# A three-product split of fp32 matmuls in the FFN's gate and up: two of the three products share weights and are issued as one of 512 columns

## The reference, cut to what matters

```
def swiglu(h, w_gate, w_up, w_down):
    return (jax.nn.silu(h @ w_gate) * (h @ w_up)) @ w_down

for layer in range(2):            # first_block; second_block has the same frame
    x = x + 0.5 * swiglu(rmsnorm(x, g0), w_gate0, w_up0, w_down0)
    x = x + mixer(rmsnorm(x, g1), ...)
    x = x + 0.5 * swiglu(rmsnorm(x, g2), w_gate1, w_up1, w_down1)
```

## Time and profile before

| | |
|---|---|
| median of 3 runs | 2746.84 us (2746.75 to 2747.86) |
| the profiled execution | 2741.84 us |
| its span, first to last instruction | 2740.0 us |
| TensorE busy | 2712.2 us, 99%, 20056 products |
| VectorE busy | 1792.1 us, 65% |
| ScalarE busy | 1430.4 us, 52% |
| GpSimd busy | 291.4 us, 11% |
| DMA | 462.02 MB, mean 169 GB/s |

### The profile page before, as it was taken

The page is one execution under the profiler, slowest core; times in us unless marked ns, Lnnn a source line. Parts: engine busy times, 40 slices in busy tenths (PEclk is TensorE's granted clock), DMA queues, the critical chain, the costliest instruction groups (busy, mean ns, idle before and its releaser), DMA issues.

```text
span 2740.0 us, 49011 instructions
## 1 busy us (share of the span) xinstructions
PE 2712.2 (99%) x20056; PEld 2564.4 (94%) x20056; DVE 1792.1 (65%) x3060; ACT 1430.4 (52%) x2445; POOL 291.4 (11%) x446
## 2 busy tenths in 40 slices
PE   9999999999999999999999999999999999999999
PEld 8999999999999999999998999999999989999998
DVE  6558776556568776556568887565565588975654
ACT  5446554444455555445447675454454476754543
POOL 0005211000005220000004011100000040211000
PEclk9999999999999999999999999999999999999999
DMA  5454334454554345445444334544544442345443
GB/s 210 185 193 159 140 142 177 188 190 171 188 191 154 139 141 185 185 170 198 186 160 168 109 131 164 185 172 185 190 179 185 166 165 108 139 169 185 162 189 142
DMA packets 64733, 462.02 MB, mean 169 GB/s; under 512 B 7296, under 2 KB 7808, under 8 KB 9344
## 3 DMA queue, kind: packets, MB, share of 16 engines
q1 hardware_dynamic: 64512, 458.90, 45.5%
HBM read 457.83 MB, written 1.05 MB: 167 GB/s over the span
## 4 chain that ended last, share of the span: by engine, by line
PE 95%; DVE 2%; POOL 2%; ACT 1%; issue 0%; DMA 0%; SPq 0%; DVEq 0%; POOLq 0%; ACTq 0%
PE bank L423 18%; PE bank L425 18%; PE bank L424 18%; PE bank L501 18%; PE bank L434 4%; PE bank L436 4%; PE bank L435 4%; PE bank L693 2%; POOL MTA L3558 1%; PE bank L605 1%; PE bank L467 1%; PE bank L1113 1%; PE bank L1058 0%; PE bank L639 0%; PE bank L965 0%
## 5 line engine op out<-in xcount | busy, mean ns | idle before, releaser
L2383 DVE TENSOR_TENSOR WLO<-RAW,WHI 128x1024 fp32r<-128x1024 f32 (+1 forms) x872 | 1048.6, 1241 | 223.2 <-ACT WHI L1468 222.5
L423 PE MATMUL bank<-XH,WHI 128*128 128x256 f32 x3712 | 1066.3, 287 | 1.5 <-ACT STB L2004 1.5
L424 PE MATMUL bank<-XL,WHI 128*128 128x256 f32 x3712 | 1051.4, 283 | 0.0
L425 PE MATMUL bank<-XH,WLO 128*128 128x256 f32 x3712 | 1051.4, 283 | 0.0
L1468 ACT CAST WHI<-RAW 128x1024 fp32r<-128x1024 f32 (+1 forms) x872 | 882.8, 1046 | 304.8 <-DMA RAW<-weights_dram 175.5
L423 PEld LDWEIGHTS bank<-XH,WHI 128*128 128x128 f32 x3712 | 712.7, 192 | 12.4 <-issue 3.8
L424 PEld LDWEIGHTS bank<-XL,WHI 128*128 128x128 f32 x3712 | 713.1, 192 | 7.0 <-issue 1.9
L425 PEld LDWEIGHTS bank<-XH,WLO 128*128 128x128 f32 x3712 | 712.7, 192 | 0.0
L1532 ACT ACTIVATE SG<-bank 128x256 f32<-128x256 f32 x152 | 58.4, 384 | 483.0 <-PE bank L425 483.0
L2496 DVE TENSOR_TENSOR HF<-SG,bank 128x256 f32<-128x256 f32 x152 | 63.9, 420 | 337.4 <-ACT SG L1532 337.4
L434 PE MATMUL bank<-WHI,XH 128*128 128x256 f32 (+2 forms) x928 | 267.3, 288 | 4.6 <-DVE XL L2437 4.5
(11 more groups left out here) (346 smaller groups left out, 3185.3 us busy)
## 6 DMA issues: line engine op xcount, KB each, us to landing
RAW<-weights_dram SPq DMA_DIRECT2D x431, 1024.0 KB, 4.8
RAW<-weights_dram SPq DMA_DIRECT2D x2, 800.0 KB, 4.2
X<-x_dram SPq DMA_DIRECT2D x2, 512.0 KB, 5.8
RAW<-weights_dram SPq DMA_DIRECT2D x2, 512.0 KB, 7.1
out_dram<-X SPq DMA_DIRECT2D x2, 512.0 KB, 2.6
RAW<-weights_dram SPq DMA_DIRECT2D x2, 384.0 KB, 3.2
CM<-mixer_dram SPq DMA_DIRECT2D x2, 320.5 KB, 9.7
CM<-mixer_dram SPq DMA_DIRECT2D x2, 176.0 KB, 5.6
```

The lines of the kernel that those rows point to most:

```text
L423: self.e.matmul(bank, h, xh[:, x0 + k, :], start=k == k0, stop=False)
L424: self.e.matmul(bank, h, xl[:, x0 + k, :], start=False, stop=False)
L425: ins = self.e.matmul(bank, l, xh[:, x0 + k, :], start=False, stop=k == k1)
L2383: e.tensor_tensor(WLO[:, c % NLO, a:b], RAW[:, c % NLO, a:b], WHI[:, c % NHI, a:b].bitcast(F32), ALU.subtract).then_inc(*up("lo", c, p))
```

## The change

1. The tokens' high and low parts lie side by side in one tile `XHL`, 512 columns per block of inputs; `XH` and `XL` are its halves.
2. `gu` calls a new helper, `beside`: per block one product of 512 columns (high weights on high and low tokens) and one of 256 (low weights on high tokens). Columns 0 to 255 of the bank hold high x high + low x high, columns 256 to 511 high x low. Gate and up now take a bank each: 4 and 5 for odd slices, 6 and 7 for even ones.
3. The halves are summed on the way out: ScalarE copies the right half to SBUF (`gcopy`, `ucopy`), VectorE adds the left half (`fg`, `fu`); `sg` and `hf` read the sums.
4. The calls of both mixers stand in another order on all four engines, and with them the order of some chunks.

```
-    XH = sb("XH", [P, 8, 256], F32R)
-    XL = sb("XL", [P, 8, 256], F32R)
+    XHL = sb("XHL", [P, 8, 512], F32R)
+    XH, XL = XHL[:, :, 0:256], XHL[:, :, 256:512]
...
+    GS = sb("GS", [P, 2, 256], F32, at_kb(24))
+    VS = sb("VS", [P, 2, 256], F32, at_kb(26))
...
+    def gu_bank(i):
+        return 4 if i % 2 else 6
...
+        def beside(self, bank, c, col, ks, xhl, k0, k1):
+            for k in ks:
+                a = col + k * P
+                h, l = WHI[:, c % NHI, a:a + P], WLO[:, c % NLO, a:a + P]
+                if k == k1:
+                    self.e.matmul(bank[:, 0:256], l, xhl[:, k, 0:256], start=False, stop=False)
+                    ins = self.e.matmul(bank[:, :], h, xhl[:, k, :], start=False, stop=True)
+                else:
+                    self.e.matmul(bank[:, :], h, xhl[:, k, :], start=k == k0, stop=False)
+                    ins = self.e.matmul(bank[:, 0:256], l, xhl[:, k, 0:256], start=False, stop=False)
+            return ins
...
         def gu(self, n, i, g, u):
-            e, c, b = self.e, ck(n, "gu", i), 5 - i % 2
-            if g == u == 0:
-                e.wait_ge(*(at("hf", n, i - 2) if i > 4 else at("ffhid", n, i - 3)))
+            e, c, b = self.e, ck(n, "gu", i), gu_bank(i) + g
             if u == 0:
+                if i > 4:
+                    e.wait_ge(*at("fg" if g == 0 else "fu", n, i - 2))
+                elif b < 7:
+                    e.wait_ge(*at("ffhid", n, b - 4))
+                else:
+                    e.wait_ge(*at("ffl", n, 2))
                 e.wait_ge(*at("lo", c, g))
-            ins = self.pairs(PS[b][:, g * 256:g * 256 + 256], c, g * 1024, range(4 * u, 4 * u + 4), XH, XL, 0, 0, 7)
+            ins = self.beside(PS[b], c, g * 1024, range(4 * u, 4 * u + 4), XHL, 0, 7)
...
+        def gcopy(self, n, i):
+            e.wait_ge(*at("gu", n, i, 0, 1))
+            e.copy(GS[:, i % 2, :], PS[gu_bank(i)][:, 256:512]).then_inc(*up("gcopy", n, i))
+        def ucopy(self, n, i):
+            e.wait_ge(*at("gu", n, i, 1, 1))
+            if i > 4:
+                e.wait_ge(*at("hf", n, i - 2))
+            e.copy(VS[:, i % 2, :], PS[gu_bank(i) + 1][:, 256:512]).then_inc(*up("ucopy", n, i))
         def sg(self, n, i):
-            e.wait_ge(*at("gu", n, i, 1, 1))
+            e.wait_ge(*at("fg", n, i))
-            e.activation(SG[:, i % 2, :], PS[5 - i % 2][:, 0:256], ACT.Silu).then_inc(*up("sg", n, i))
+            e.activation(SG[:, i % 2, :], GS[:, i % 2, :], ACT.Silu).then_inc(*up("sg", n, i))
...
+        def fg(self, n, i):
+            e.wait_ge(*at("gcopy", n, i))
+            e.tensor_tensor(GS[:, r, :], GS[:, r, :], PS[gu_bank(i)][:, 0:256], ALU.add).then_inc(*up("fg", n, i))
+        def fu(self, n, i):
+            e.wait_ge(*at("ucopy", n, i))
+            e.tensor_tensor(VS[:, r, :], VS[:, r, :], PS[gu_bank(i) + 1][:, 0:256], ALU.add).then_inc(*up("fu", n, i))
...
-M2_ORDER = [("bt", 0), ("bt", 1), ("bt", 2), ("bt", 3), ("bx", 9), ("bq", 0), ("bq", 1), ("bq", 2), ("bk", 0), ("bx", 0), ("bx", 10),
+M2_ORDER = [("bt", 0), ("bt", 1), ("bt", 2), ("bt", 3), ("bx", 9), ("bq", 0), ("bq", 1), ("bx", 0), ("bq", 2), ("bx", 10), ("bk", 0),
```

More of the change, by code:

```diff
@@ L747, in m1 @@
             self.ptr(n, 9)
+            self.at_(n, 12, 0, 0)
+            self.at_(n, 12, 0, 1)
+            self.at_(n, 12, 1, 0)
+            self.at_(n, 12, 1, 1)
+            self.at_(n, 5, 0, 0)
+            self.sc(n, 0, 0)
+            self.sc(n, 0, 1)
+            self.at_(n, 5, 0, 1)
+            self.at_(n, 5, 1, 0)
+            self.at_(n, 5, 1, 1)
             self.at_(n, 10, 0, 0)
@@ L1577, in ffn @@
             self.ffh(n, 2)
+            self.gcopy(n, 3)
             self.sg(n, 3)
+            self.ucopy(n, 3)
             self.hh(n, 3)
@@ L1581, in ffn @@
             self.hi(c + 7, 1)
-            for m in range(2, 11):
+            for m in range(2, 10):
                 k = c + 3 * m
-                if m < 10:
-                    self.hi(k + 2, 0)
-                else:
-                    self.hi(k + 1, 1)
+                self.hi(k + 2, 0)
+                self.gcopy(n, 2 * m)
                 self.sg(n, 2 * m)
+                self.ucopy(n, 2 * m)
                 self.hh(n, 2 * m)
-                if m < 10:
-                    self.hi(k + 2, 1)
-                    self.sg(n, 2 * m + 1)
-                    self.hi(k + 3, 0)
-                    self.hh(n, 2 * m + 1)
-                    self.hi(k + 3, 1)
-                    self.hi(k + 4, 0)
-                    if m < 9:
-                        self.hi(k + 4, 1)
-                else:
-                    self.hi(k + 2, 0)
-                    self.hi(k + 2, 1)
-                    self.sg(n, 21)
-                    self.hh(n, 21)
+                self.hi(k + 2, 1)
+                self.gcopy(n, 2 * m + 1)
+                self.sg(n, 2 * m + 1)
+                self.hi(k + 3, 0)
+                self.ucopy(n, 2 * m + 1)
+                self.hh(n, 2 * m + 1)
+                self.hi(k + 3, 1)
+                self.hi(k + 4, 0)
+                if m < 9:
+                    self.hi(k + 4, 1)
                 if n == 0 and 4 <= m < 8:
                     self.tab(1 + (m - 4) // 2, m % 2)
-            self.hi(first[n + 1], 0)
-            self.hi(first[n + 1], 1)
+            self.gcopy(n, 20)
+            self.hi(c + 31, 1)
+            self.sg(n, 20)
+            self.hi(c + 32, 0)
+            self.ucopy(n, 20)
+            self.gcopy(n, 21)
+            self.hh(n, 20)
+            self.hi(c + 32, 1)
+            self.sg(n, 21)
+            self.ucopy(n, 21)
+            self.hi(c + 33, 0)
+            self.hh(n, 21)
+            self.hi(c + 33, 1)
         def psq(self, n, j):
@@ L2546, in ffn @@
             self.lo(c + 7, 1)
[L2547 removed]
+            for m in range(2, 10):
                 k = c + 3 * m
[L2549 to L2552 removed]
+                self.lo(k + 2, 0)
+                self.fg(n, 2 * m)
+                self.fu(n, 2 * m)
                 self.hf(n, 2 * m)
                 self.hl(n, 2 * m)
[L2555 to L2568 removed]
+                self.lo(k + 2, 1)
+                self.fg(n, 2 * m + 1)
+                self.fu(n, 2 * m + 1)
+                self.hf(n, 2 * m + 1)
+                self.hl(n, 2 * m + 1)
+                self.lo(k + 3, 0)
+                self.lo(k + 3, 1)
+                if m < 9:
+                    self.lo(k + 4, 0)
+                    self.lo(k + 4, 1)
                 if n == 0 and 3 <= m < 7:
                     self.ang(1 + (m - 3) // 2, (m - 3) % 2)
[L2571 to L2572 removed]
+            self.fg(n, 20)
+            self.lo(c + 31, 0)
+            self.lo(c + 31, 1)
+            self.fu(n, 20)
+            self.hf(n, 20)
+            self.lo(c + 32, 0)
+            self.hl(n, 20)
+            self.fg(n, 21)
+            self.lo(c + 32, 1)
+            self.fu(n, 21)
+            self.hf(n, 21)
+            self.lo(c + 33, 0)
+            self.hl(n, 21)
+            self.lo(c + 33, 1)
         def lam1(self, n):
@@ L2780, in m1 @@
             self.xt(n, 1, 3)
+            self.lo(c + 3, 0)
+            self.lo(c + 3, 1)
             self.lo(c + 4, 0)
```

759 lines of the change are left out of this document (367 added, 392 removed), and 2 rows, old and new, of the table M2_TRANSPOSED.

## The result

| | before | after |
|---|---|---|
| median, same chip, 4 runs each | 2747.35 us (2746.75 to 2748.38) | 2715.54 us (2714.0 to 2716.94) |
| ratio | | 0.989 (95% interval 0.9876 to 0.9904) |
| span of the profiled execution | 2740.0 us | 2712.1 us |

The change makes the kernel 31.8 us faster; the forecast said 37.4 us less and 2709 us, and its range of 2697 to 2724 holds the result. By the medians the sum was 6 us too large. By the profiled executions (2741.84 and 2714.0 us) the gain is 27.8 us, and the sum 10 us too large: the four runs of before behind the median of 2747.35 lie 5 us above its profiled execution, and in later rounds before's median came at 2744.55, 2743.23 and 2741.36 us. Where the sum was off, the views tell.

What follows compares the result with a forecast made beforehand. TensorE's list of products was taken to bound the kernel. Gate and up 30.4, mixer 2 2 x 3 and mixer 1 2 x 0.5 us sum to 37.4 off 2741.84, giving 2704.4; with 5.0 for the median, 2709 us, range 2697 to 2724.

Steps and rivals of the forecast that it cites:

- the 30.4 us: Gate and up of all FFNs: 12.5 ns saved at each of 2432 places by joining two products that share weights.
- The place: One block's products in gate or up: 359.4 ns before, 347 ns forecast after, one of 512 and one of 256 columns.
- The bounds (340 and 355 ns): Cheapest and dearest cost of a block's wide and narrow product in gate and up: 47.2 or 11.2 us saved in all.
- a place costs over 352: Sign of being wrong: one block's products in a gate or up slice cost over 352 or under 342 ns.
- most of the fixed part does not go: Rival, gate and up: a wide product between narrow ones stays dear, place 355 ns, 11.2 us saved, 2729 us; chance 0.08.
- The chain's cover: Draining gate's bank: 13.3 us until its next use (8.3 for last slices) against a 3.1 us chain, so costed at nothing.
- 7 forecast: Both mixers, two runs each: net 3 us gained per run of mixer 2 and 0.5 us per run of mixer 1.
- one of GpSimd's two rope chains is over by then: Mixer 2: bx 10 ahead of the key products lets a rope end early, so the 7.0 us of key-transpose waits go.
- the dearer waits: Possible new waits: mixer 2's second key transposes and first mpt, up to 1.5 us each; mixer 1's sc 0 mask, about 1.
- The mixers gave something: Answers the rival that the mixers give nothing, their waits moving instead of going: 2716 to 2720 us; chance 0.12.
- the banks came in time: Answers the rival that gate and up wait for late bank drains, making the kernel slower: 2752 us and up; chance 0.03.
- the product became no dearer than its rows allow: Answers the rival that the change does not do what it says, through a dearer product: time about as now; chance 0.02.

Runs made afterwards that it cites:

- W: Letter of the probe orders: W is a product of 512 columns, N one of 256; pure streams cost 227 and 120 ns.
- double_copies: The change with each of its 304 ScalarE copies out of a bank made twice; 2715.12 us, 0.9892 of before (the change: 2715.54 us).
- mixers_only: The kernel before with only the new order of the mixers' calls, gate and up as before; 2734.42 us, 0.9964 of before.
- runs of four: One FFN with four wide, then four narrow products, otherwise as the change; place 349.7 ns, FFN 186.51 us against 186.68 in the change.
- W W N N: One FFN with two wide, then two narrow products, otherwise as the change; place 348.1 ns, FFN 185.43 us against 186.69 for alternating products.
- probe: The change with another product order in each of the eight FFNs, the eighth with an added partial product; 2743.26 us. Its sixth interleaves gate and up: place 351.3 ns.
- fold: The change with every second block of gate and up turned round, so widths run W N N W; 2706.13 us, 0.9862 of before (the change: 0.989).
- probe2: The change with a second set of product orders, one per FFN, three of them wide, narrow, narrow, wide; 2708.88 us.

## Why the prediction was right, and what in it was not

The forecast of the total held, but not by its own parts alone. Gate and up gave 18.1 of the 30.4 us. What made up for most of the difference is not in the working: 2.8 us in the down products, 1.1 us in the first FFN's start, and 4 us by which the medians lie farther apart than the profiled executions. That the total came within 6 us is in part luck.

**The place: right in kind, too large in size.** The step was "I take 347 ns, the settled 512 (227, between 225 and 229) with a settled 256 (120)". The pure streams have exactly these prices (226.9 and 120.0), but in the change's alternation neither width settles: 235.1 + 117.3 = 352.4 ns. The gain is 7.5 ns per place in place of 12.5 (18.1 us), plus 0.3 us per FFN in the down products, which the working had not counted, and the 1.1 us in the first FFN. 22.0 us stand for 30.4. The bounds (340 and 355 ns) held, but of the prediction's own signs of being wrong one came: "a place costs over 352", by 0.4 ns. By the place the rival "most of the fixed part does not go", at 355, was nearer to the truth than the forecast's own value; by the total (2729 us) it was not. Its argument, the first two behind a change at 235 ns, gives W; its counterpart in the same rows, 256 behind 512 at 115, was read as the end of a debt. The two together, 235 + 115 = 350, would have been 1.9 ns per place from what the slice measured; settling between the two corners of the bounds instead of on the mean of what stands next to a change was the error. By the isolated distance in the Trainium skill, TensorE: Matmul & The Clock Gate, section Back-to-back issue gap, 2.5 ns per place would have gone. The starts give three times that.

**The drain: right.** No wait on the new steps, and twice the copies cost nothing (`double_copies`). The lengths were sized about right: the copies add up to 111.1 us (362 and 369 ns each, for 384) and the additions to 127.3 us, and the SiLU, which now reads `GS`, takes 418 ns for 384. The busy times grew by less, 107.1 and 116.9 us for 117 and 128, since busy time is a union and counts what overlaps once. The chain's cover was read from a stretch of 16.51 us taken for the period of two slices and two down steps; that period is 17.0 us (102.99 to 119.99), so the cover is half a microsecond longer than the working has it. The copies:

```profile
L1555 ACT COPY GS<-bank 128x256 f32<-128x256 f32 x152 | 56.1, 369 | 120.4 <-PE bank L442 120.4
L1562 ACT COPY VS<-bank 128x256 f32<-128x256 f32 x152 | 55.0, 362 | 8.8 <-PE bank L442 8.7
```

**The mixers: the sum right, its parts not.** 6.1 us in the profiled execution, for 7 forecast. About 1.2 of them are the clock's: before has 6.8 us at the lower level in its second mixer 2 and the change 3.4, and at equal clock mixer 2 gives about 2.5 us, not 3.7. In mixer 2 the wait of 3.5 us went as said, but the working let the rope end early ("one of GpSimd's two rope chains is over by then"); one of them became the new wait of 1.8 us, and 3.5 - 1.8 = 1.7 us is about what equal clocks show. None of the dearer waits that it priced came. ScalarE's 1.5 us for `STB`, most of which was to go with the 7.0, stayed whole. In mixer 1 the working counted 0.5 us for `STA`, which got worse by 1.1 us over two runs (2.3 for 1.2), and held the end of the mixer for unmoved, where `MTA` and `XL` gave 2.0 us each. With the 0.9 us more for `GT` that is 2.0 us by the waits, 2.4 by the lengths. TensorE's calls are unmoved there, but in VectorE's list a conversion that stood ahead of the first of the last steps (`mg`) stands behind it.

**The range and the other rivals.** Half of the way to each end is 20.8 to 38.8 us for gate and up and, with the mixers' bounds, 0.5 to 9.5 for them; that is 21 to 48 us, where the text has 22 to 50. The mixers gave something (`mixers_only`), the banks came in time, and the product became no dearer than its rows allow.

## What to carry to other kernels

Two products that share weights are worth joining where each carries a fixed part: here 120 + 120 ns became 235, with the drain free on idle engines. When that leaves products of two widths, try their order, and time the whole stage: W N N W has the same products and buffers as W N W N and took 1.25 us less in each FFN, while runs of four gave 0.2. Before you judge an edit by the profiled length of a stage with many short waits, set the granted clock of both traces beside it.

## What the runs showed of the hardware

**Alternating widths mostly have a beat.** In the order W N W N the distances repeat over three places: 233, 117, 241, 120, 236 and 113 ns. In W W N N they are 234, 236, 116, 112 and 233, 231, 113, 119. In the last two slices of `probe`'s sixth FFN, with neighbours in different banks and no down products ahead, W N W N has no beat: 229 to 231 and 115 to 118 ns. What makes the beat, no run told; only that the tile is not it, and that neighbours in different banks do not always prevent it.

**GpSimd and VectorE stretch each other.** VectorE's conversions and GpSimd's rope in after, the same 128x1024 conversion without GpSimd at work and beside it:

```profile
1459.42 3.48 DVE L2427 TENSOR_TENSOR WLO<-RAW,WHI 128x1024 fp32r<-128x1024 f32 x3
...
1469.41 5.09 DVE L2427 TENSOR_TENSOR WLO<-RAW,WHI 128x1024 fp32r<-128x1024 f32 x3
```

Three conversions in 3.48 us alone, in 5.09 us beside GpSimd, whose own step went from 1.30 to 2.12 us. So in these traces the chains of both engines are longer where the order lets them meet, and a distance worked out from rows where they ran alone is too short.

**The clock falls inside a kernel that is 99% busy.** In the second mixer the granted clock goes from its upper level (2.4 GHz) to the lower (1.2 GHz) for 3.4 or 6.8 us and back. In before this came behind the wait of 3.5 us (columns: window, length, PE, PEld, DVE, ACT, POOL, granted clock, DMA share, GB/s):

```profile
1486.60:1490.00 3.40, 0.00 (x0) 0.00 (x0) 3.16 (x9) 0.00 (x0) 1.80 (x2) 1.00 0.21 87
1490.20:1493.60 3.40, 3.40 (x17) 3.40 (x18) 3.40 (x3) 0.69 (x1) 3.31 (x3) 0.50 0.01 2
```

In after, behind the wait of 1.8 us:

```profile
1474.10:1477.60 3.50, 3.50 (x16) 3.27 (x15) 2.63 (x2) 2.51 (x4) 3.42 (x2) 0.51 0.05 12
```

In `fold`, with TensorE busy throughout and 96-column products in its stream, and the same stretch of after, which held the upper level:

```profile
1430.00:1436.80 6.80, 6.80 (x34) 6.80 (x34) 5.14 (x12) 4.68 (x9) 3.56 (x9) 0.50 0.40 157
```

```profile
1430.00:1436.80 6.80, 6.80 (x62) 6.74 (x61) 5.23 (x20) 5.74 (x12) 0.00 (x0) 1.00 0.67 271
```

So each 3.4 us at the lower level cost about 1.5 us, and some of them came right behind a wait. A wait does not always bring one: the second 3.5 us wait of before was followed by a fall in the first execution and by none in the second, and the change's 1.8 us wait by one fall in four (two executions, two mixers each). Where the falls lie varies from one execution of a kernel to the next (before: first mixer 2 once with 3.4 and once with 13.6 us), so part of the mixers' small gains and losses is not the order's. Whether `fold`'s fall at 1430, which all three executions with its FFNs and the change's mixer 2 had, and `probe2` too, belongs to that kernel or came by chance stays open: one of the change's two executions had a shorter one there as well.
